# A state-space mixer's recurrence over 256 steps, done in 64 chunks of 4 steps

## The reference, cut to what matters

```
u = (h @ w_in).reshape(bsz, seq, 32, 16)
dt = exp(log_dt);  mag = exp(lr * dt)
abar = mag * (cos(li * dt) + i sin(li * dt))         # one complex number per group and state
bbar = ((abar - 1) / (lr + i li)) * b                # per group: 64 states x 16 channels
bu[t] = einsum('bsgc,gpc->bsgp', u, bbar)
xs[t] = abar * xs[t-1] + bu[t]                       # associative_scan over the 256 steps
y = einsum(xs_re, c_re) - einsum(xs_im, c_im) + d_skip * u
z = gelu(y);  z = z * sigmoid(z @ w_glu);  mix = z @ w_out
```

## Time and profile before

| | us |
|---|---|
| median of 3 runs (1462.62 to 1466.22) | 1465.23 |
| the profiled execution | 1465.11 |
| its span | 1463.2 |
| PE busy | 1304.6 |
| DVE busy | 964.6 |
| ACT busy | 645.9 |
| POOL busy | 594.4 |

### The profile page before, as it was taken

How to read it: one execution, slowest core, us unless ns; L and a number is a source line. 1 busy time by engine, 2 the same in 40 slices (tenths; PEclk the granted TensorE clock), 3 DMA queues, 4 the chain that set the end, 5 groups by cost and what they waited for, 6 DMA issues and landing times.

```text
span 1463.2 us, 21621 instructions
## 1 busy us (share of the span) xinstructions
PE 1304.6 (89%) x7938; PEld 1128.6 (77%) x7943; DVE 964.6 (66%) x1461; ACT 645.9 (44%) x1067; POOL 594.4 (41%) x367
## 2 busy tenths in 40 slices
PE   2378799998979989999899999898999876899998
PEld 2234699997856679999788888798888865799998
DVE  7998633334593553333473766568999987489997
ACT  4301444444424544444445544345444442355554
POOL 6499344444450244444435422133323321344552
PEclk9788999999986989999989999999999998999999
DMA  7000466663600446666437533253344430456563
GB/s 236 1 29 29 142 203 189 184 186 110 202 29 1 147 147 193 189 186 184 137 101 235 168 98 92 71 141 119 116 142 128 131 115 29 129 159 191 184 195 120
DMA packets 170406, 197.09 MB, mean 135 GB/s; under 512 B 14050, under 2 KB 135398, under 8 KB 170342
## 3 DMA queue, kind: packets, MB, share of 16 engines
q1 hardware_dynamic: 169115, 192.03, 43.0%
q10 hardware_dynamic: 1226, 4.21, 0.9%
HBM read 195.17 MB, written 1.05 MB: 134 GB/s over the span
## 4 chain that ended last, share of the span: by engine, by line
PE 67%; DVE 21%; POOL 4%; issue 3%; ACT 3%; DMA 1%; DVEq 0%; ACTq 0%; SPq 0%; POOLq 0%
PE acc L650 21%; PE wk L605 11%; PE wk L606 11%; PE wk L607 11%; DVE LO L441 2%; DVE arena L2229 2%; PE wk L882 2%; DVE arena L2177 1%; DVE arena L2213 1%; PE acc L605 1%; DVE arena L2241 1%; PE wk L1003 1%; POOL y L535 1%; PE acc L1029 1%; PE acc L607 1%
## 5 line engine op out<-in xcount | busy, mean ns | idle before, releaser
L441 POOL TENSOR_TENSOR LO<-raw,HI 128x1024 fp32r<-128x1024 f32 (+3 forms) x191 | 460.4, 2416 | 774.5 <-ACT HI L1243 774.2
L1243 ACT ACTIVATE HI<-raw 128x1024 fp32r<-128x1024 f32 (+3 forms) x382 | 364.8, 995 | 162.1 <-PE acc L650 72.2
L605 PE MATMUL wk<-XH,HI 128*128 128x256 f32 x1296 | 374.4, 289 | 24.6 <-POOL LO L441 12.6
L606 PE MATMUL wk<-XL,HI 128*128 128x256 f32 x1296 | 370.6, 286 | 0.0
L607 PE MATMUL wk<-XH,LO 128*128 128x256 f32 x1296 | 370.1, 286 | 0.0
L441 DVE TENSOR_TENSOR LO<-raw,HI 128x1024 fp32r<-128x1024 f32 (+3 forms) x191 | 240.1, 1259 | 167.1 <-ACT HI L1243 166.8
L605 PEld LDWEIGHTS wk<-XH,HI 128*128 128x128 f32 x1296 | 252.6, 195 | 32.0 <-issue 27.9
L606 PEld LDWEIGHTS wk<-XL,HI 128*128 128x128 f32 x1296 | 252.8, 195 | 2.1
L607 PEld LDWEIGHTS wk<-XH,LO 128*128 128x128 f32 x1296 | 252.6, 195 | 0.0
L650 PE MATMUL acc<-HI,HH 128*128 128x512 f32 x424 | 133.2, 395 | 14.6 <-DVE HL L2220 13.9
L650 PE MATMUL acc<-LO,HH 128*128 128x512 f32 x424 | 131.9, 392 | 0.0
(11 more groups left out here) (315 smaller groups left out, 2023.2 us busy)
## 6 DMA issues: line engine op xcount, KB each, us to landing
raw<-in_mlp_w SPq DMA_DIRECT2D x128, 512.0 KB, 4.1
raw<-in_w_in SPq DMA_DIRECT2D x100, 512.0 KB, 4.0
raw<-in_w_up SPq DMA_DIRECT2D x44, 512.0 KB, 3.9
raw<-in_w_down SPq DMA_DIRECT2D x44, 256.0 KB, 3.1
raw<-in_att_w_in SPq DMA_DIRECT2D x16, 512.0 KB, 4.1
raw<-in_w_ssd_proj SPq DMA_DIRECT2D x16, 512.0 KB, 3.6
raw<-in_att_w_out SPq DMA_DIRECT2D x8, 512.0 KB, 4.2
raw<-in_w_out SPq DMA_DIRECT2D x8, 512.0 KB, 3.7
```

Of the source, the lines that this page charges most:

```text
L441: tensor_tensor(LO[:, s, cs], raw[:, s % 2, "ab".index(part), 0:m], HI[:, s, cs].bitcast(F32), ALU.subtract).then_inc(S(f"lo_{part}"), 1)
L605: mm(o, lh, rh, start=start, stop=False, skip_group_check=skip)
L606: mm(o, lh, rl, start=False, stop=False, skip_group_check=skip)
L1243: A(HI[:, s, j * m:(j + 1) * m], raw[:, s % 2, j, 0:m], ACT.Copy).then_inc(S(f"hi_{part}"), 1)
```

## The change

The 256 steps become 64 chunks (`NC`) of 4 steps (`CL`). From tables of the powers 0 to 4 of the transition (`pw5`), DVE builds `w5`, which takes a chunk's 4 x 16 inputs of a group to the state at the chunk's end, and `cq5`, which takes a state to the 4 x 16 outputs after it. `u5` holds the input with the 4 steps of a chunk and 32 channels of a pair on the partitions, chunks along the free axis. PE multiplies (`drive`), DVE scans over 64 chunks for four pairs at once, one quarter `q` of the pairs at a time (`scanned`), with `mag4` = magnitude to the fourth power and 0 at each pair's first chunk. The part within a chunk is a block-triangular 128 x 128 matrix per pair, `m5`, which PE makes (`kernels5`, with the skip term in it), ACT copies out and POOL completes with zeros; `within` multiplies it by `u5`, and `carried` adds what the scanned states bring. Gelu comes after all four quarters, in 16 instructions on 32 partitions each, which also bring the steps back in order. The phase table `e5` has 64 entries per pair, from sine instead of doubling. In the stages before, the first half of the norm's product (`pre_block`) stands ahead of the small vectors on DVE, the copy of piece 0 stands ahead of the transposed input's on ACT, `hi_to(3)` and `hi_to(4)` move, and POOL zeroes `w5` and `cq5` first of all. `ssm_d` is loaded in four DMAs of 16 x 32 instead of one of 4 x 128. Code after the mixer is the same.

```diff
 # POOL
+            G.memset(w5[:, :, :, :], 0.0)
+            G.memset(cq5[:, :, :, :], 0.0).then_inc(S("zero5_ready"), 1)
             row_rstd(0)
-            turn_table(G, steps.link, E_SPLIT, ST, ..., 1, 64)
             upto(1)
-            turn_table(G, steps.link, E_SPLIT, ST, etmp[:, E_SPLIT * P:], 64, SEQ - 1)
+            pool.wait_ge(S("mag5_ready"), 1)
+            pool.wait_ge(S("q5_ready"), 1)
+            G.memset(mag4[:, :, 0:1], 0.0)
+            G.tensor_copy(mag4[:, :, 1:NC], sm5[:, 10, :].unsqueeze(2).to_broadcast([P, ST, NC - 1]))
+            pool.wait_ge(S("kk_psum"), 1)
+            for k in range(3):
+                G.memset(m5[32 * k:32 * k + 32, :, 0:32 * (3 - k)], 0.0).then_inc(S("m5_zero"), 1)
             upto(3)
-            ...the sums and products of the 16 pairs
+            upto(4)
 # PE
+            for g in range(8):
+                inputs_turned(g)          # 4 transposes of w5 each, waits bt_ready >= g - 1
+            for q in range(4):
+                drive(q)                  # 8 products of 64 columns, weights 128x128
+            for q in range(4):
+                last = kernels5(q)        # 8 products of 128 columns and one for the skip term
+            last.then_inc(S("kk_psum"), 1)
+            pe.wait_ge(S("m5_ready"), 1)
+            for q in range(4):
+                within(q)                 # 4 products of 64 columns
+            for q in range(4):
+                carried(q)                # waits x5_ready >= q + 1; 8 products of 63 columns
+            glu_slot = arrived()
+            for k in range(3):
+                glu(glu_slot, k)
 # ACT
+            hi_to(0)
             xT_high(0)
             hi_to(1)
...
+                for k in range(CL):
+                    for j in range(4):
+                        last = A(quarters(u5)[32 * k:32 * k + 32, 2 * b:2 * b + 2, j, :], ...wk[32 * j:...], ACT.Copy)
...
+            for r in range(2):
+                for q in range(4):
+                    act.wait_ge(S("bt_psum"), 4 * r + q + 1)
+                    A(wt5[:, r, 4 * q:4 * q + 4, :], wk[:, 2 + q % 2, :]..., ACT.Copy).then_inc(S("bt_ready"), 1)
+                last = A(w5[:, r, :, 32:]..., w5[:, r, :, 0:32]..., ACT.Copy)
+            last.then_inc(S("bb_ready"), 1)
...                                       # e5: Abs, Sin, Sin, Copy on 1024 elements each
+            act.wait_ge(S("kk_psum"), 1)
+            for k in range(CL):
+                last = A(m5[ks, :, 32 * s:P], kk[ks, :, 0:P - 32 * s], ACT.Copy)
+            last.then_inc(S("m5_ready"), 1)
+            hi_to(4)
+            act.wait_ge(S("x5_used"), 4)
+            for j in range(4):
+                for t in range(CL):
+                    last = A(zf[32 * j:..., t], yc[32 * t:32 * t + 32, :, j, :], ACT.Gelu_apprx_tanh)
 # DVE
+            def scanned(q):
+                if q >= 2:
+                    dve.wait_ge(S("x5_used"), q - 1)
+                TT(planes(ra), bu, ea, ALU.mult)
+                link(TT(planes(rb), bu, eb, ALU.mult))
+                TT(ra[:, 0:256], ra[:, 0:256], ra[:, 256:512], ALU.add)
+                link(TT(rb[:, 0:256], rb[:, 256:512], rb[:, 0:256], ALU.subtract))
+                V.tensor_tensor_scan(z[:, 0:256], mag, ra[:, 0:256], 0.0, ALU.mult, ALU.add)
+                link(V.tensor_tensor_scan(z[:, 256:512], mag, rb[:, 0:256], 0.0, ALU.mult, ALU.add))
+                TT(planes(ra), planes(z), ea, ALU.mult)
+                link(TT(planes(rb), planes(z), eb, ALU.mult))
+                TT(ra[:, 0:256], ra[:, 0:256], ra[:, 256:512], ALU.subtract)
+                TT(rb[:, 0:256], rb[:, 0:256], rb[:, 256:512], ALU.add).then_inc(S("x5_ready"), 1)
+            for q in range(4):
+                scanned(q)
+                if q in (1, 2):
+                    lo_next()
+            lo_to(4)
```

425 lines of the change are left out of this document (218 added, 207 removed).

## The result

The changed kernel takes 1450.79 us (median of 4 runs, 1447.53 to 1451.44) against 1463.92 for the kernel before in the same comparison: a ratio of 0.9897, 95% interval 0.9881 to 0.9914. That is some 13 to 15 us gained where 37 were forecast, and it lies outside the range. Its profiled execution has a span of 1449.4 us.

A forecast was written before the change was run, and what follows sets the result against it. PE bounds most of the span, but DVE and POOL the stage up to the gate; its steps ended the gate at 112.7 us instead of 149.6, so 1465.1 - 36.9 = 1428. Range 1416 to 1438; 8 in 10, 1412 to 1445.

The forecast's parts named there:

- step 1: Start to the first weight product: 30.0 us instead of 30.94, with two DVE stalls beside POOL's low parts.
- rival C: POOL's fill runs at 2.3 ns an element: 13.6 us later from the first step on, 1442; chance 0.04.
- A: No stall at the start, small instructions slip past POOL: 4.6 us less, 1423; chance 0.16.
- step 3: ACT makes `u5` and the tables: `u5` copies 0.19 us apart, 3.0 us; all done at 55.1 us.
- B: PE stays at the low level through the stage: 160 passes cost 0.09 more, 14 us, 1442; chance 0.12.
- step 4: PE's input terms and matrices: transposes, not counted as activity, leave PE cold; `drive` 9.2 us, `kernels5` 8.6, to 72.9.
- step 5: New wait while ACT copies `m5`, 4.6 us to 77.6; then `within` 5.3, first `carried` 1.9, to 84.9.
- step 6: DVE's last two quarters: 5.3 us each, the first of them waiting for `x5_used`; last `carried` 2.8, to 99.5.
- step 7: To the gate's end: 16 gelus on the path, 4.9 us at 0.30 each; gate product 7.2, to 112.7.
- Rival E: The change does not pay: ACT's 32 copies, 16 gelus and 4 `m5` copies need 4 times theirs; chance 0.03.
- Gate and covers: Gate product without overlap, 48 passes, 7.2 us; waits `q5_ready` and `e5_ready` covered with 4 us of room.
- Behind the gate: After the gate product the same work follows, PE-bound from `down` on, its length changing by no more than 1 us.

The follow-up runs named there:

- Experiment 3: The changed kernel with other forms of ACT's small input copies, 23 for 32, values wrong; only spacing counts: 0.16 us apart on the same quadrant, 0.28 where it changes.
- Experiment 1: The changed kernel with 31 products of a zero block added on PE between the groups of transposes ahead of `drive`: 1436.17 us, ratio 0.981.
- experiment 5: The changed kernel with 31 zero products ahead of `drive`, and more ahead of `within` and around the `carried` groups: 1435.65 us, ratio 0.9817.
- experiment 2: The changed kernel with gelu's output in the order (step, chunk), written without a step, time order restored by later reads: 1447.26 us, ratio 0.9878.
- experiment 9: The changed kernel with 23 zero products on PE ahead of the turning of the first MLP's input: 1444.56 us, ratio 0.987.

## Why the prediction was wrong, step by step

- **Start (step 1): right.** 30.97 for 30.0. POOL's fills took 3.51 and 4.37 us, 0.855 ns an element, so rival C falls. Both stalls beside POOL's low parts came (2.24 us at 17.69, 2.05 at 21.70), so A falls. The small vectors began at 12.54, not 11.1, as the column copies came later than I had them.
- **ACT's small copies (step 3): this term was mis-sized.** "I take that partitions don't matter" picked the lower of the two bounds, 0.19; the upper, 0.31 without overlap, was nearer to the measured 0.28. Experiment 3 names the reason, the change of quadrant. 1.5 us.
- **The rate of PE (steps 4 and 5): this is the step that failed.** I took 0.12 us a pass and 16 passes of 0.21 "until PE speeds up, as it did 3.4 us after its start". That row was of 256-column passes; the 64 passes of `drive` never sped up. (Nor does the profile give a low clock for that row: it has 1.00 for all of the first 40 us, before and after, though the first passes stand 0.21 apart. Only later, as in the changed kernel's gate product from 126.5 to 129.8 us, do 0.21 and a clock of 0.50 stand together.) I gave B 14 us at a chance of 0.12. It came, for the most part: all 64 passes of `drive`, some 24 of the 72 of `kernels5`, and all of `within` and of the two groups of `carried` on the path ran low. These took 10.75 us more than the forecast's, and the exchange some 1.6. So B's price was about right, and its chance too small. Experiment 1 shows that the level was the whole of it for `drive` and `kernels5` (7.3 and 8.1 us, where the forecast had 9.2 and 8.6), and experiment 5 for `within` (3.79 in place of 7.09) and `carried`.
- **The transposes ahead of `drive` (step 4).** The forecast that they leave PE at the low level came true, but not by the rule given for it: the clock was at 0.50 before the last 24 of the 32 began. Experiment 3 speaks against the rule. There it fell during them, at 51 us, and was back at 1.00 from 54.5, though PE had done nothing but transposes since 45.2.
- **The wait for `m5` (step 5): right**, 5.04 for the sum's 4.7, released by ACT.
- **DVE's quarters (step 6): right**, 5.4 us a quarter for 5.3, and the third began behind the first `carried`, after 13.86 us of idle time.
- **Gelu (step 7): mis-sized by a factor of two**, 0.62 for 0.30. Of the 5 us 3.7 are the step in its output (experiment 2). The other 1.3 fit the overlap that copies lose when they change quadrant (experiment 3); for gelu itself no run takes it apart. Rival E named such a cost, but asked for a factor of four to matter. It needed to be added to B.
- **Gate and covers: right.** The gate took 7.3 us for 7.2, and neither `q5_ready` nor `e5_ready` ended last.
- **Behind the gate: wrong by 2.1 us.** "Behind the gate the same work follows" held for the work and not for PE's level at the first MLP's weights (experiment 9).
- **The range** reached up to 1445 for B and C, at 1442 each and each alone. B and the dear ACT instructions came together: 1428, 21.1 up to the gate's end and 2.1 behind it give 1451, and 1450.8 was measured. PE's level (12.4) and ACT's instructions (6.6) are 19 of these 23 us; take away either of the two and the time lies inside the range.

## What to carry to other kernels

When work is moved from a busy stage to TensorE, price its passes at the low level of the clock first, and ask of each wait ahead of them how long TensorE idles in it: here an idle time of 5 us cost 10 us behind it, and 31 products of zeros, in time that was idle anyway, kept the level up. Price small ScalarE instructions by their full length wherever two neighbours start on different quadrants, and take 1.6 to 1.7 times that length where SBUF is read or written with a step as large as here. And since the same layer took 158 to 166 us in twelve profiles by its own clock, judge an edit by the time at the end of its stage and by the whole of several executions, both; one profile's difference of 5 us far behind the edit says nothing about it.

## What the runs showed of the hardware that I had not expected

- At the low level 64-column fp32 passes with 128x128 weights stood 0.214 us apart and at the high one 0.112, so the number of columns hardly entered: 128-column ones stood 0.22 and 0.11 apart. Sixty-four of them without a gap, 13.7 us, did not raise the level; behind them it rose during the 128-column ones, some 5 us in.
- ScalarE: 160 ns + 0.835 ns an element (32x512 in 587 ns, 32x2048 in 1870), 0.11 us of overlap between neighbouring copies where both read and write started on the same partition as before, and none where either had changed (0.16 against 0.28 us apart for 128 elements).
- ScalarE, a step of 16 bytes in an SBUF output: 609 ns for 256 elements against 375; a step of 256 bytes in an SBUF input: 1086 ns for 512 against some 630. A step of 16 bytes in a PSUM input: nothing.
- VectorE is held for the rest of a GpSimd subtraction, some 2.1 us a time, not only on small vectors but in scans and sums of 256 and 512 elements, all of them with their inputs in SBUF.
